# The last pair's down projection, scatter and sums by halves of the features; the output in four pieces

## What is computed

```python
for i in range(DEPTH):                      # DEPTH = 2
    h = rmsnorm(x, ln_mix[i])
    qkv = h @ w_qkv[i]
    ...                                     # attention gives o
    x = x + o @ w_o[i]
    x = x + hier_moe(rmsnorm(x, ln_ffn[i]), w_group[i], w_expert[i], w1[i], w3[i], w2[i])

# in hier_moe, with t (256, 1024), combine (256, 16) mostly zero:
for e in range(N_EXPERTS):                  # w1, w3: 1024x512, w2: 512x1024 for each expert
    h = jax.nn.silu(t @ w1[e]) * (t @ w3[e])
    y = y + combine[:, e:e + 1] * (h @ w2[e])
```

## Time and profile before

| | |
|---|---|
| time, median of 3 runs | 674.86 us (673.85 to 676.22) |
| the profiled execution | 675.01 us |
| its span | 673.2 us |
| granted TensorE clock, mean | 0.989 of full |
| PE, PEld busy | 639.0 us (95%), 283.6 us (42%) |
| DVE, ACT, POOL busy | 202.7, 177.0, 71.1 us |
| moved by DMA | 229.61 MB, mean 341 GB/s |
| chain that ended last | PE 79%, DMA 9%, DVE 5% |

### The profile page before, as it was taken

How to read it: one execution, slowest core, us unless ns; L and a number is a source line. 1 busy time by engine, 2 the same in 40 slices (tenths; PEclk the granted TensorE clock), 3 DMA queues, 4 the chain that set the end, 5 groups by cost and what they waited for, 6 DMA issues and landing times.

```text
span 673.2 us, 7941 instructions
## 1 busy us (share of the span) xinstructions
PE 639.0 (95%) x2947; PEld 283.6 (42%) x2947; DVE 202.7 (30%) x614; ACT 177.0 (26%) x425; POOL 71.1 (11%) x85
## 2 busy tenths in 40 slices
PE   8999899899999999999999887998999999999996
PEld 5444445633433433432354444455344344334332
DVE  1655433512302302301243655234113113113112
ACT  2126642302212112112131554321212112112112
POOL 0006550000000000000010576200000000000000
PEclk9999999899999999999999999997999999999998
DMA  8999706579997999999999993484999799999993
GB/s 323 277 295 422 274 1 272 227 312 421 422 423 294 424 421 423 421 422 421 403 295 249 411 406 79 147 364 153 423 421 422 318 401 421 422 423 423 422 423 125
DMA packets 42882, 229.61 MB, mean 341 GB/s; under 512 B 8207, under 2 KB 8497, under 8 KB 18274
## 3 DMA queue, kind: packets, MB, share of 16 engines
q1 hardware_dynamic: 41212, 224.66, 85.0%
q0 software_dynamic: 1312, 4.23, 2.0%
q10 hardware_dynamic: 326, 0.31, 0.2%
HBM read 228.10 MB, written 1.08 MB: 340 GB/s over the span
## 4 chain that ended last, share of the span: by engine, by line
PE 79%; DMA 9%; DVE 5%; POOL 2%; ACT 2%; issue 1%; SPq 0%; DVEq 0%; POOLq 0%; ACTq 0%
PE ps L1304 28%; PE ps L1331 15%; PE ps L1086 11%; DMA attw<-in_w_dram 8%; PE ps L1168 6%; PE ps L1271 5%; PE ps L1283 4%; POOL attw L413 2%; PE ps L1121 2%; PE ps L1150 2%; PE ps L1137 1%; PE ps L1235 1%; DVE attw L799 1%; PE ps L1313 1%; DMA ring<-in_ln_mix_dram 1%
## 5 line engine op out<-in xcount | busy, mean ns | idle before, releaser
L1304 PE MATMUL ps<-attw,work 128*64 128x512 f32 x512 | 111.7, 592 | 1.5 <-DMA attw<-in_w_dram 1.5
L1304 PE MATMUL ps<-ring,work 128*64 128x512 f32 x512 | 111.4, 593 | 0.0
L1086 PE MATMUL ps<-attw,work 128*128 128x512 f32 x192 | 88.2, 603 | 0.3 <-DVE work L695 0.3
L1331 PE MATMUL ps<-ring,work 128*64 128x512 f32 x384 | 85.7, 595 | 1.1
L931 DVE COPY work<-ps 32x512 f32<-32x512 f32 x64 | 43.7, 683 | 106.1 <-PE ps L1331 105.7
L923 DVE TENSOR_TENSOR work<-work,ps 128x512 f32<-128x512 f32 x16 | 11.0, 688 | 190.3 <-PE ps L1304 190.3
L1304 PEld LDWEIGHTS ps<-attw,work 128*64 128x64 f32 x512 | 36.7, 137 | 75.1 <-issue 71.6
L1304 PEld LDWEIGHTS ps<-ring,work 128*64 128x64 f32 x512 | 36.5, 137 | 72.4 <-issue 72.3
L601 ACT COPY work<-ps 32x512 f32<-32x512 f32 x64 | 36.9, 576 | 107.3 <-PE ps L1331 106.9
L413 POOL TENSOR_SCALAR attw<-attw,stat 128x256 f32<-128x256 f32 x64 | 58.8, 932 | 50.2 <-DVE stat L814 50.0
L1168 PE MATMUL ps<-attw,work 128*128 128x512 f32 x128 | 59.7, 601 | 0.7 <-issue 0.5
(11 more groups left out here) (149 smaller groups left out, 486.4 us busy)
## 6 DMA issues: line engine op xcount, KB each, us to landing
ring<-in_w_dram SPq DMA_DIRECT2D x112, 1024.0 KB, 17.9
attw<-in_w_dram SPq DMA_DIRECT2D x80, 1024.0 KB, 17.5
attw<-in_w_qkv_dram SPq DMA_DIRECT2D x4, 2048.0 KB, 21.0
attw<-in_w_o_dram SPq DMA_DIRECT2D x8, 1024.0 KB, 22.6
attw<-in_w_qkv_dram SPq DMA_DIRECT2D x4, 1024.0 KB, 15.5
ring<-bias_rows POOLq DMA_DIRECT2D x16, 256.0 KB, 6.9
x_sb<-in_x_dram SPq DMA_DIRECT2D x2, 512.0 KB, 6.3
out_dram<-x_sb SPq DMA_DIRECT2D x2, 512.0 KB, 3.6
```

Source lines behind the costliest of these rows:

```text
L1086: last = pe.matmul(ps[:, g, :], xT[:, k, P * tt:P * tt + P], wqkv[part][:, k, :], start=(k == 0), stop=(k == KB - 1))
L1304: last = pe.matmul(ps[64 * e:64 * e + 64, 6 + which, :], xg[:, k, c:c + 2 * SLOTS], w13(which, k // 4)[:, e, k % 4, :], start=(k == 0), st ...
L1331: last = pe.matmul(ps[64 * e:64 * e + 64, half, :], hT[:, k, 64 * e:64 * e + 64], w2(kh)[:, e, k % 2, 512 * half:512 * half + 512], start= ...
```

## The change

In the last pair of each layer the down projection goes half by half: `down(0, 0)`, `down(1, 0)`, then `down(0, 1)`, `down(1, 1)`. New semaphores `half_done`, `y0_half` and `y1_half` let the y copies and the final scatter go by halves too. `tile_summed` and `half_summed` tell of each scattered half, and the x copies are dealt out anew: DVE takes features 0 to 511 of both tiles, ACT features 512 to 1023 of tile 0 and, in the first layer, of tile 1; in the second layer DVE takes the last one as well. The filler matmuls around the final scatter are gone. The output leaves in four pieces of 128 rows of 2 KB, three issued by SP and one by ACT. The next layer's transposes wait for the new order of copies. ACT's last pair stands outside of its loop.

```diff
@@ sync
-            for tt in range(TT):
-                if tt == 0:
-                    sp.wait_ge(moe_out_dve, 2 * DEPTH)
-                else:
-                    sp.wait_ge(moe_out_act, 2 * DEPTH)
-                sp.dma_start(out.rearrange("b (t p) d -> p (b t) d", p=P)[:, tt, :],
-                             x_sb[:, tt, :]).then_inc(out_written, 16)
-            sp.wait_ge(out_written, 16 * TT)
+            for n, (tt, half) in enumerate(((0, 0), (1, 0), (1, 1))):
+                sp.wait_ge(moe_out_dve, 2 * DEPTH - 1 + n)
+                sp.dma_start(out[0, P * tt:P * tt + P, 512 * half:512 * half + 512],
+                             x_sb[:, tt, 512 * half:512 * half + 512]).then_inc(out_written, 16)
+            sp.wait_ge(out_written, 16 * 2 * TT)
@@ scalar
-                        act.wait_ge(m.w2_used, 3 * n + 2 + half + m.credit)
+                        if last and half == 0:
+                            act.wait_ge(m.half_done, R + 1)
+                        else:
+                            act.wait_ge(m.w2_used, 3 * n + 2 + half + m.credit)
...
+                        if last and half == 0:
+                            ins.then_inc(m.y1_half, 1)
+                    ins.then_inc(m.y1_copied, 1)
+
+                with act.Fori(0, PAIRS - 1) as i:
                     moe_pair(main, L, i)
+                moe_pair(main, L, PAIRS - 1, last=True)
...
-                act.wait_ge(main.scattered, PAIRS * (L + 1))
-                for half in range(2):
-                    act.copy(x_sb[:, 1, 512 * half:512 * half + 512], ps[:, sum_bank(1, half), :]).then_inc(moe_out_act, 1)
+                act.wait_ge(tile_summed, 2 * L + 2)
+                act.copy(x_sb[:, 0, 512:D], ps[:, sum_bank(0, 1), :]).then_inc(moe_out_act, 1)
+                if L + 1 < DEPTH:
+                    act.wait_ge(main.scattered, PAIRS * (L + 1))
+                    act.copy(x_sb[:, 1, 512:D], ps[:, sum_bank(1, 1), :]).then_inc(moe_out_act, 1)
+            act.wait_ge(moe_out_act, 2 * DEPTH - 1)
+            act.dma_start(out[0, 0:P, 512:D], x_sb[:, 0, 512:D]).then_inc(out_written, 16)
@@ vector
-                    dve.wait_ge(m.w2_used, 3 * n + 2 + half + m.credit)
+                    if last and half == 0:
+                        dve.wait_ge(m.half_done, R + 1)
+                    else:
+                        dve.wait_ge(m.w2_used, 3 * n + 2 + half + m.credit)
...
-                dve.wait_ge(tile_summed, L + 1)
-                for half in range(2):
-                    dve.tensor_copy(x_sb[:, 0, 512 * half:512 * half + 512], ps[:, sum_bank(0, half), :]).then_inc(moe_out_dve, 1)
+                dve.wait_ge(tile_summed, 2 * L + 1)
+                dve.tensor_copy(x_sb[:, 0, 0:512], ps[:, sum_bank(0, 0), :]).then_inc(moe_out_dve, 1)
+                dve.wait_ge(half_summed, L + 1)
+                dve.tensor_copy(x_sb[:, 1, 0:512], ps[:, sum_bank(1, 0), :]).then_inc(moe_out_dve, 1)
+                if L + 1 == DEPTH:
+                    dve.wait_ge(main.scattered, PAIRS * (L + 1))
+                    dve.tensor_copy(x_sb[:, 1, 512:D], ps[:, sum_bank(1, 1), :]).then_inc(moe_out_dve, 1)
@@ tensor
-                        pe.wait_ge(moe_out_act if tt else moe_out_dve, 2 * L - 1 + kh)
+                        pe.wait_ge(moe_out_act if kh else moe_out_dve, 2 * L - 1 + tt)
...
-                    pe.wait_ge(m.y0_copied, n)
-                    pe.wait_ge(m.y1_copied, n)
                     for half in range(2):
+                        if final and half == 0:
+                            pe.wait_ge(m.y0_half, L + 1)
+                            pe.wait_ge(m.y1_half, L + 1)
+                        elif final or half == 0:
+                            pe.wait_ge(m.y0_copied, n)
+                            pe.wait_ge(m.y1_copied, n)
...
+                    if last_pair:
+                        pe.wait_ge(m.ht_copied, 2 * n + 2)
+                        landed(5)
+                        down(1, 0).then_inc(m.half_done, 1)
+                        pe.wait_ge(m.pct_copied, n + 1)
+                        down(0, 1).then_inc(m.w2_used, 1)
+                        down(1, 1).then_inc(m.w2_used, 2)
+                        return
...
-                stay_awake(5)
                 scatter(main, PAIRS * (L + 1), final=True)
-                if L + 1 < DEPTH:
-                    stay_awake(4)
```

More of the change, by code:

```diff
@@ L216, in encoder @@
         pos_done, routed, flag_ready = sem("pos_done"), sem("routed"), sem("flag_ready")
-        tile_summed = sem("tile_summed")
+        tile_summed, half_summed = sem("tile_summed"), sem("half_summed")
         seeded, x_scaled = sem("seeded"), sem("x_scaled")
@@ L245, in __init__ @@
                 self.scattered = sem(tag + "scattered")
+                self.half_done = sem(tag + "half_done")
+                self.y0_half = sem(tag + "y0_half")
+                self.y1_half = sem(tag + "y1_half")
                 self.credit = credit
@@ L584, in _, with moe_pair @@
                         act.activation(rt[9][:, 0:TT], rt[9][:, 0:TT], ACT.Exp).then_inc(exp_out, 1)
-                def moe_pair(m, R, i):
+                def moe_pair(m, R, i, last=False):
                     n = PAIRS * R + i
@@ L597, in moe_pair @@
                     for half in range(2):
-                        act.wait_ge(m.w2_used, 3 * n + 2 + half + m.credit)
+                        if last and half == 0:
+                            act.wait_ge(m.half_done, R + 1)
+                        else:
+                            act.wait_ge(m.w2_used, 3 * n + 2 + half + m.credit)
                         for e in range(2):
                             to, of = SLOTS * (2 + e), SLOTS * (2 * e + 1)
-                            last = act.copy(y_sb[to:to + SLOTS, 512 * half:512 * half + 512], ps[of:of + SLOTS, half, :])
-                    last.then_inc(m.y1_copied, 1)
-                with act.Fori(0, PAIRS) as i:
+                            ins = act.copy(y_sb[to:to + SLOTS, 512 * half:512 * half + 512], ps[of:of + SLOTS, half, :])
+                        if last and half == 0:
+                            ins.then_inc(m.y1_half, 1)
+                    ins.then_inc(m.y1_copied, 1)
+                with act.Fori(0, PAIRS - 1) as i:
                     moe_pair(main, L, i)
+                moe_pair(main, L, PAIRS - 1, last=True)
                 with act.If(more_rounds(act, L) > 0):
                     with act.Fori(0, ROUNDS - 1) as r:
-                        with act.Fori(0, PAIRS) as i:
+                        with act.Fori(0, PAIRS - 1) as i:
                             moe_pair(extra[L], r, i)
+                        moe_pair(extra[L], r, PAIRS - 1, last=True)
                     act.wait_ge(extra[L].scattered, (ROUNDS - 1) * PAIRS)
-                act.wait_ge(main.scattered, PAIRS * (L + 1))
-                for half in range(2):
-                    act.copy(x_sb[:, 1, 512 * half:512 * half + 512], ps[:, sum_bank(1, half), :]).then_inc(moe_out_act, 1)
+                act.wait_ge(tile_summed, 2 * L + 2)
[5 more added lines that the diff above has]
+            act.dma_start(out[0, 0:P, 512:D], x_sb[:, 0, 512:D]).then_inc(out_written, 16)
         @block.vector
@@ L931, in moe_pair @@
                         ins = dve.tensor_copy(y_sb[to:to + SLOTS, 512 * half:512 * half + 512], ps[of:of + SLOTS, half, :])
+                    if last and half == 0:
+                        ins.then_inc(m.y0_half, 1)
                 ins.then_inc(m.y0_copied, 1)
@@ L1284, in scatter @@
                                              start=False, stop=False, skip_group_check=True, tile_position=(2 * SLOTS * tt, 0))
-                            if final and half and tt == 0:
+                            if final and tt == 0:
                                 last.then_inc(tile_summed, 1)
+                            elif final and half == 0:
+                                last.then_inc(half_summed, 1)
                     last.then_inc(m.scattered, 1)
```

## The result

The change made the kernel slower by 0.3%: the ratio of its time to that of the kernel before is 1.0032 (95% interval 1.0018 to 1.0046; medians 676.12 and 674.01 us, 20 runs each). Forecast was 1.5 us less; measured are 2.1 us more. The span of the profiled execution is 675.6 us against 673.2.

| stretch, us | before | after | forecast |
|---|---|---|---|
| start to the first expert matmul | 133.8 | 133.4 | as before |
| to the first projection matmul of layer 2 | 205.6 | 205.5 | 205.2 |
| to the first expert matmul of layer 2 | 124.9 | 125.3 | as before |
| to the landing of the last pair's unit 5 | 195.6 | 196.9 | 195.6 |
| to the end of the down projection | 3.8 | 5.5 | 5.5 |

The account below looks back on a forecast made before the run. TensorE and the weight stream were taken to run neck and neck, followed by a serial tail. From 675.0 us, -0.4 at the layer boundary and -1.1 at the end gave 673.5, range 671.6 to 676.9.

Parts of the forecast that it names:

- The wait for unit 5: Each layer's last down projection: PE waits 1.8 us for w2 rows 256 to 511, ending the projection 1.7 us later.
- "I count 0" for the code: ACT's program grows by one pair outside its loop; claimed cost 0 us.
- The filler matmuls: time saved nothing: Around the final scatter: the five fillers take 1.38 us under a copy, so removing them saves no time.
- The output: Kernel end: four pieces, issued from 667.5, finish landing at 671.7, 1.1 us before today's; bounds 0.5 to 1.4 gained.
- fixed cost of 1.9 us and common rate: Output landing: each piece has about 1.9 us fixed cost, and the 1 MB streams in 2.45 us.
- 671.3 among the signs: Kernel end: the forecast would show the last output issued near 668.5 and landing near 671.3 of the span.
- The boundary: From first layer's end to second layer's first projection matmul: gain 0.4 us; bounds 0.8 and -0.2.
- the halving doesn't hide 1.4 us of copy: Layer tail: forecast said halving hides 0.86 us of scatter and 1.4 of copy, the wait taking 1.8 back.
- SP's gate of w_o: First layer's end: w_o load gate met at 333.6, not 329.8; backlog absorbs it, cost 0, at most 2.7 us.
- The clock rival: PE's clock falls after its new waits, 1.7 us per fall: one gives 675.2 (chance 0.20), two 676.9 (0.08).
- The rival "unit 5 is in time": Last pair's down projection: PE does not wait in either layer, total 670.0; chance 0.05.

Follow-up runs that it names:

- e5: Changed kernel with one expert's 1 MB of each layer's last-pair w2 load left out, so unit 5 lands earlier; ratio to the kernel before 0.994.
- e9: Kernel before with only the order of the last pair's down projections changed; ratio 1.0063, 4.2 us slower.
- e11: The changed kernel measured once more, beside e12 on one chip; ratio to the kernel before 1.0019.
- e12: e2 measured again (changed kernel, down projections in the old order), beside e11 on one chip; ratio to the kernel before 0.9963.
- e7: Kernel before with only ACT's last pair written outside of its loop; ratio 0.999.
- e8: e2 with all of ACT's pairs kept in one loop; ratio to the kernel before 0.9945.
- e10: Kernel before without its five and four filler matmuls around the final scatter; ratio 1.0031, 2.1 us slower.
- e13: Kernel before with its filler matmuls cut from 128 columns to one, same number of instructions; ratio 0.9993.
- e6: Control for e5: kernel before with the same 1 MB per layer left out; ratio 1.0008.
- e1: Changed kernel with the output as before, two DMAs of 512 KB on SP; ratio to the kernel before 1.0016.
- e3: Changed kernel with both the old down-projection order and the old two-piece output; ratio to the kernel before 0.9945.
- e4: Kernel before with only its output changed to four pieces of 256 KB; ratio 0.9994.
- e2: Changed kernel with the last pair's down projections in the old order, all else as changed; ratio to the kernel before 0.9932.
- e15: Changed kernel with filler matmuls of one column put back where the fillers were; ratio to the kernel before 1.0003.
- e14: Changed kernel with the old down-projection order and one-column filler matmuls where the fillers were; ratio to the kernel before 0.9967.
- e16: e2 with nine one-column matmuls added at the start of PE's program; ratio to the kernel before 0.9976.
- e17: e2 with four one-column matmuls added at the start of PE's program; ratio to the kernel before 0.9966.

## Why the prediction was wrong, step by step

**The wait for unit 5: right.** Forecast 1.8 us per layer, measured 1.70 and 1.66, in the place named, with the end of the projection 1.7 us later and half 0 of y no earlier. e5 and e9 confirm it by taking it away and by making it alone. Its price by the ratios is 3.8 us (e11 against e12), 4.2 (e9), 6.2 (after against e5); the two waits in a profile are 3.4 of it, and the rest isn't explained.

**"I count 0" for the code: wrong, 1.3 us.** This is the step that failed. I had looked at ACT's program and at the time of a first instruction behind a loop, that is at an engine waiting for its code. What shows in the profiles is the other end: the fetch occupies one DMA engine, and in a stage where the weight stream is the bound, everything behind it is late, 1.3 us in the changed kernel. And ACT's program was the wrong one to look at (e7, e8): PE's moved the packet. "The filler matmuls: time saved nothing" left the same thing out: without them the kernel is 2.1 us slower (e10), though only 1.0 us of that is traced to the fetch. That the 1.3 us are in the time and not only in the profile isn't shown (e13).

**The output: mis-sized, by 2.2 us in the profile.** The issues came where I had them (668.75 for a forecast of 668.7 after the later landing, the last at 669.98 for 670.1). My fixed cost of 1.9 us and common rate would have had the last piece there 2.2 us before it was. The rate is common only while all DMA engines have work; one was behind by 28 packets of 2 KB, after an instruction packet had run in the middle of the output. So this term, too, lacked the code: the sum had nothing in the output's way. The trail isn't peculiar to the four pieces: e6, e7 and e10 have the packet and the trail with two, two-piece kernels had their last landing between 4.1 and 5.8 us after the first output issue, and the ratios of e1, e3 and e4 tell no difference in either direction. Part of it was the kernel before, whose profile had a quick end: 9.2 us from the end of the projection to the last landing, where e9, e13, e6, e10 and e7, also with two pieces behind a whole scatter, have 8.9 to 10.7. The forecast's own numbers for the last landing differ as well: 671.85 by the stream, 671.7 taken without a reason, 671.3 among the signs.

**The boundary: 0.1 for 0.4.** Counted from PE's start on unit 5, scatter, copies and the transposes of h1 came within 0.1 us of the forecast. The transposes of h0 and DVE's copy of them came 0.1 to 0.2 us later than I put them, the first matmul 0.2. That was in my bounds. With the wait gone the boundary gives 1.7 to 1.8 us: from the end of the projection to the next layer's matmul it takes 4.0 to 4.1 us in e2, e3 and e12 against 5.8 before. One sentence of the working is wrong, though not the times around it: the halving doesn't hide 1.4 us of copy. Before, too, only the copy of half 1 stands behind the projection; what is gained is half a scatter, 0.86 us, and 1.7 less 0.86 is the 0.8 us that the sums come later.

**SP's gate of w_o: right.** SP starts on these loads at 333.28 in place of 330.96 and is done with them at 340.7 in place of 341.1; PE never waits for w_o.

**The clock rival: didn't happen.** Ten waits of 1.6 to 1.7 us for unit 5 (after, e1, e9, e11, e15), each preceded and followed by full matmuls, all at clock 1.00 to the next idle time. Changed kernel, second layer:

```profile
659.50:661.20 1.70, 0.05 (x2) 0.02 (x1) 0.00 (x0) 0.00 (x0) 0.00 (x0) 1.00 0.03 14
661.20:666.50 5.30, 5.29 (x24) 1.94 (x24) 1.36 (x2) 1.15 (x2) 0.00 (x0) 1.00 0.00 0
```

The time, 676.1, lies between the rival's 675.2 and 676.9, for another reason. The Trainium skill ("TensorE: Matmul & The Clock Gate", section Why this matters for your kernels) advises against idle gaps between bursts of matmuls, but against longer ones than these. The ten waits between dense matmuls agree with that, without a fall. The 1.8 us of the earlier trace rows don't: there the clock was at 0.50 from 129.9, with thin work in front of the gap, and PE busy for 0.77 of the 1.5 us behind it. So the page was no ground to expect a fall here.

**The rival "unit 5 is in time"** gave 670.0 as its price for an unhindered halving, 5.0 us under before. The kernels that have it and the halving (e2, e3, e8, e12, e14, e16, e17) are at 0.9932 to 0.9976, 1.6 to 4.6 us under.

**Open.** Which engine's program the 16 KB packet holds and what places it: it moves with PE's instructions (e10, e13, e16) and in one case with SP's (e6). What a fetch in the stream costs in medians: the stretch says 1.2 us, but e13 and e14 don't tell it from nothing. How far the spread between e2 and e12 is the chip. Why the output trails by more than the instruction packet takes, and how often a packet falls into it.

## What to carry to other kernels

Before an order of work is changed for the sake of what comes after, ask for each operand when it lands: here the old order hid a transfer that arrived just in time, and the new one asked for it 1.7 us sooner to make something ready that could not be ready sooner. A split by halves pays at the end of a serial tail (1.6 to 4.6 us here, with the filler gone), if the halves are taken from the work behind the last landing. And where a DMA stream is the bound, or an output ends the kernel, code counts as traffic: look at the instruction queue's packets before and after, since adding or removing instructions that cost no time of their own can move a fetch from a pause into the stream. Here that is plain in the profiles and not settled in the total time.

## What the runs showed of the hardware

A fetch of 16 KB of instructions took about 1.04 us of one of the 16 DMA engines. Where it fell into the full weight stream (twelve kernels of seventeen), unit 5 landed 0.9 to 1.5 us later than before. Where it fell into the output (twelve profiles of nineteen), the last packets trailed by 1.2 to 2.4 us, in the changed kernel one of 2 KB at a time, at 29 GB/s. Matmuls of one column aren't free for PE: eight records took 1.05 us, of which their weight loads were busy for 0.97 us in e14 and e15, while ten of 128 columns took 1.38.
